# Expert down weights issued by ScalarE: a sparse-attention and mixture-of-experts step on one Trainium2 core

## What is computed

```python
def swiglu(x, w13, w2):
    a, b = jnp.split(x @ w13, 2, axis=-1)
    return (jax.nn.silu(a) * b) @ w2

    ...
    y = swiglu(h, w_sh13, w_sh2)
    for e in range(N_EXPERTS):          # 64
        y = y + combine[:, e:e + 1] * swiglu(h, w_exp13[e], w_exp2[e])
```

## Time and profile before

| | us |
|---|---|
| three runs | 1360.8, 1352.27, 1358.23 |
| median | 1358.23 |
| the profiled execution | 1353.77 |
| its span, first to last instruction | 1352.1 |

### The profile page before, as it was taken

One profiled execution on the slowest core, in us unless ns is written; L12 is line 12 of the kernel. 1 busy time (PEld: TensorE's weight loads), 2 busy tenths in 40 slices (PEclk: granted clock), 3 DMA queues, 4 the chain that ended last, 5 costly groups with the idle time before them and its releaser, 6 DMA issues. The chain is left out here.

```text
span 1352.1 us, 20742 instructions
## 1 busy us (share of the span) xinstructions
PE 1232.7 (91%) x7495; PEld 517.5 (38%) x7495; DVE 636.8 (47%) x1114; ACT 230.0 (17%) x496; POOL 453.8 (34%) x574
## 2 busy tenths in 40 slices
PE   5999889999999798999899998989989899988997
PEld 3545443444555544554232222222222222222343
DVE  1336579969971533674332222223323332221775
ACT  1024331021233310011011110111101101101211
POOL 5444416312244000154444343443434344431010
PEclk9999988999999898999999998999989999989899
DMA  8233220122111266024689999999999999997971
GB/s 281 60 112 106 65 82 9 63 74 86 24 25 24 83 234 261 35 70 167 244 333 415 402 415 411 399 412 395 415 388 412 398 405 399 413 408 270 400 176 54
DMA packets 98107, 318.65 MB, mean 236 GB/s; under 512 B 51642, under 2 KB 53438, under 8 KB 80025
## 3 DMA queue, kind: packets, MB, share of 16 engines
q1 hardware_dynamic: 74960, 269.94, 51.7%
q0 software_dynamic: 22960, 47.45, 10.1%
q10 hardware_dynamic: 96, 0.02, 0.0%
HBM read 298.70 MB, written 31.33 MB: 244 GB/s over the span
## 5 line engine op out<-in xcount | busy, mean ns | idle before, releaser
L1675 PE MATMUL ps<-arena 128*32 128x512 f32 x3072 | 355.4, 616 | 45.0 <-DMA arena<-in_w_exp 41.5
L2160 DVE STREAM_TRANSPOSE arena<-arena 128x1024 f32<-128x1024 f32 x48 | 100.0, 2083 | 253.9 <-DMA arena<-h_rows,arena 252.8
L997 POOL DMA_INDIRECT arena<-h_rows,arena x192 | 193.0, 1005 | 73.0 <-issue 72.1
L1675 PEld LDWEIGHTS ps<-arena 128*32 128x32 f32 x3072 | 97.6, 113 | 266.7 <-issue 214.3
L1688 PE MATMUL ps<-arena 128*32 128x512 f32 x1536 | 173.5, 592 | 0.8 <-DVE arena L2194 0.8
L1334 PE MATMUL ps<-arena 128*128 128x512 f32 (+1 forms) x384 | 166.5, 591 | 4.9 <-DMA arena<-in_w_in 4.8
L1056 ACT ACTIVATE arena<-ps 128x512 f32<-128x512 f32 (+5 forms) x226 | 102.5, 485 | 364.4 <-PE ps L1310 202.1
L1004 POOL DMA_INDIRECT y_rows<-arena x48 | 48.7, 1015 | 303.9 <-DVE arena L2194 289.1
L1334 PEld LDWEIGHTS ps<-arena 128*128 128x128 f32 x384 | 72.5, 192 | 91.4 <-issue 90.7
L1688 PEld LDWEIGHTS ps<-arena 128*32 128x32 f32 x1536 | 49.5, 110 | 115.5 <-issue 115.5
L1265 ACT ACTIVATE arena<-ps 128x256 f32<-128x256 f32 x48 | 18.4, 384 | 390.3 <-PE ps L1675 390.3
(11 more groups left out here) (237 smaller groups left out, 1294.3 us busy)
## 6 DMA issues: line engine op xcount, KB each, us to landing
arena<-in_w_exp SPq DMA_DIRECT2D x64, 2048.0 KB, 21.2
arena<-in_w_exp SPq DMA_DIRECT2D x64, 1024.0 KB, 15.8
arena<-in_w_in SPq DMA_DIRECT2D x6, 2048.0 KB, 8.0
arena<-y_rows SPq DMA_DIRECT2D x5, 2048.0 KB, 12.1
arena<-y_rows SPq DMA_DIRECT2D x5, 1024.0 KB, 7.9
arena<-in_x_prompt SPq DMA_DIRECT2D x8, 512.0 KB, 9.0
arena<-in_cache_v SPq DMA_DIRECT2D x128, 32.0 KB, 1.8
arena<-in_w_out SPq DMA_DIRECT2D x2, 2048.0 KB, 11.9
```

Source lines behind the costliest of these rows:

```text
L997: pool.indirect_dma_start(out=xg[s][:, 256 * g:256 * g + 256], out_offset=None, in_=h_quarters, in_offset=bass.IndirectOffsetOnAxis(ap=fro ...
L1675: ins = mm(ps[e % 3][q, :], xgT[e % 2][:, kk, q], w13[slots[g]][:, kk, :], start=(kk == 0), stop=(kk == KT - 1))
L2160: v.transpose(xgT[e % 2].rearrange("p c (g i) -> p g c i", g=4), xg[e % 3].rearrange("p (g j c) -> p g c j", g=4, c=KT)).then_inc(turned, 1)
```

## The change

`up_weights` and `down_weights` move up in the file so that two engines can use them. On SyncE, `load_expert` becomes `load_up`, which issues only the up weights; the first three main experts' down weights and the first kept one's are still issued there (those of the second kept expert too, by a line that did not change). On ScalarE, after its half of the y eviction of pass e, come the down weights of main expert e + 3, and in every third pass those of the next kept expert too. The slot is free then, because that eviction has waited for the down product of pass e. Instructions that compute are the same ones.

```diff
-            def load_expert(e, s, passes):
+            def load_up(e, s, passes):
                 if passes:
                     sp.wait_ge(up, passes)
                 sp.dma_start(*up_weights(e, s)).then_inc(w13_in[s], 16)
-                if passes:
-                    sp.wait_ge(down, passes)
-                sp.dma_start(*down_weights(e, s)).then_inc(w2_in[s], 16)
 
             def load_main(n):
-                load_expert(4 * (n // 3) + n % 3, main_slot(n)[0], n - 2 if n >= 3 else 0)
+                load_up(4 * (n // 3) + n % 3, main_slot(n)[0], n - 2 if n >= 3 else 0)
+                if n < 3:
+                    sp.dma_start(*down_weights(n, main_slot(n)[0])).then_inc(w2_in[main_slot(n)[0]], 16)
 
             def load_kept(q):
-                load_expert(4 * q + 3, kept_slot(q)[0], 3 * q - 3 if q >= 2 else 0)
+                load_up(4 * q + 3, kept_slot(q)[0], 3 * q - 3 if q >= 2 else 0)
+                if q < 1:
+                    sp.dma_start(*down_weights(3, kept_slot(q)[0])).then_inc(w2_in[kept_slot(q)[0]], 16)
...
                 copy(ye[e % 2][:, 0:512], ps[3 + 2 * (e % 2)][:, :], scale=gate[:, list_row(e):list_row(e) + 1]).then_inc(ya, 1)
+                if e + 3 < PASSES:
+                    slot = main_slot(e + 3)[0]
+                    act.dma_start(*down_weights(4 * ((e + 3) // 3) + e % 3, slot)).then_inc(w2_in[slot], 16)
+                if e % 3 == 2 and (e + 4) // 3 < PASSES // 3:
+                    q = (e + 4) // 3
+                    slot = kept_slot(q)[0]
+                    act.dma_start(*down_weights(4 * q + 3, slot)).then_inc(w2_in[slot], 16)
```

More of the change, by code:

```diff
@@ L713, in load_values, with up_weights, down_weights @@
             load_pages(eng, b, (("cache_v", lambda g: values[b // 4][:, bass.ds(b % 4 * NPG + g, 1), :][:, 0, :]),), v_in[b // 4])
+        def up_weights(e, s):
+            return w13[s], a["w_exp13"][0][e:e + 1].rearrange("a (p k) n -> p (a k) n", p=P)
+        def down_weights(e, s):
+            return w2[s], a["w_exp2"][0][e:e + 1].rearrange("a (p k) n -> p (a k) n", p=P)
         block = ctx.enter_context(nc.Block())
```

## The result

The changed kernel takes 1390.3 us (median), the kernel before 1355.72 us in the runs beside it: a ratio of 1.0261, 95% interval 1.0207 to 1.0315. The change makes the kernel 2.6% slower, outside the range of the prediction and on the side of its second rival. The profiled execution took 1388.8 us, 35.0 more than that of before.

The account below looks back on a forecast made before the run. DMA engines were taken to bound the passes, 11.95 us at best against 12.32. Passes at 12.14 give 7.6 us off; issue cost and starting lead count zero, so -8 us from 1358.23 gives 1350 us, range 1336 to 1378.

Parts of the forecast that it names:

- second rival: In the passes, gathers become the limit (d over 3.1): 1358 to 1435 us, mostly under 1378; chance 0.26.
- Issue cost: 59 down loads issued on ScalarE behind its y half fit under an up product of 6.89 us: zero.
- The price of a turn: At the DMA queues, a POOL packet beside both loaded weight queues takes 0.93 us a turn.
- The prediction's own sign of being wrong: In the passes, if gathers land past 15 us, the pass grows beyond 12.6 us.
- TensorE then waits about 1.3 us in every pass: TensorE waits this for VectorE, instead of 5 us in every third pass for weights.
- that goes: On TensorE, the slow up product after long weight waits, 8.73 us against 7.07, disappears, inside the same sum.
- 12.14: Forecast us a pass, taken as the middle between 12.33 and the floor of 11.95; 7.6 us off in 42 passes.
- d of 3.1: Gathers later by d us make a pass at least 11.3 + d/3; 3.1, the worst of three batches, gives 12.33.
- The loop of 33.9 us: Gather loop from scatter issue through transpose, turn, up, down and y half: 33.9 us for three passes, 11.3 a pass.
- hand layout: Queue loads laid out by hand for three passes at 12.4 us: d 3.1 for the worst batch, 0.9 for the mean.
- The whole bound of 8.8: Gathers 8.8 us later if both weight queues are always loaded: 14.2 us a pass, over 1435 us.
- The rule: Issuing DMAs from several engines saves issue time only: sum 0, time 1358 us; as the rival "nothing changes", chance 0.10.

Follow-up runs that it names:

- e1: The changed kernel with down loads given back to SyncE's queue, requests at the same moments: 1346.97 us, 0.992 of the kernel before; run again, 1346.59 us, 0.9938.
- filler: The changed kernel with 20 more transposes of a constant on TensorE ahead of the turn in every third pass: 1365.57 us, 1.0044 of the kernel before.
- e7: The one-queue kernel of e1 with weight loads in pieces of 4 KB a partition: 1364.44 us, 1.006 of the kernel before.

## Why the prediction was wrong

**Right.** The bound before was right: DMA engines with a floor of 11.95 us a pass and dips behind waits; e1 takes the dips and runs at 12.11. Issue cost nothing: ScalarE's copies lost 3.8 us to the issues in front of them, in 14 cases, and no engine waited for that. The waits on weights went altogether. The price of a turn held to 0.01 us, and gathers landed 4.5 us later. The prediction's own sign of being wrong came, gathers past 15 us (15.3) and a pass beyond 12.6 (13.05). The second rival named the mechanism, the place and the side.

**Wrong, the decisive step: "TensorE then waits about 1.3 us in every pass".** It waits 3.5 to 6.9 us in every third, and "that goes", said of the slow up product, did not come true: the slow up products moved from behind the weight waits to behind the late turns, and there are more of them. Behind the 14 late turns the up product takes 8.65 us on the mean to the next row (9.13 in the cycle above), against 6.89, and most of these turns take 0.19 more. 13 of them lie in the 42 passes: 25 us, and no term of the sum held it. The kernel before has 14 us of the same there, behind 8 weight waits, so of the 30.7 us that the change costs in these passes the clock has 11; against a forecast that put it at nothing it is all 25. The filler, which takes most of this away and leaves the late gathers, gives 1.0261 - 1.0044 of 1356 us back, 29 us, and 20.4 in the traces' 42 passes. I had the slow up products of the kernel before in the rows, and took it for granted that waits would spread.

**Wrong, the choice of 12.14.** It was the middle between the worst of three batches (d of 3.1, 12.33 a pass) and their mean (0.9). A batch's loop closes three passes later, on the batch of the same place in the cycle of kept loads. So the worst batch meets itself and sets the pace; the mean of the three has no part in it. The worst place, the first of the three above, has 22.3 us from scatter issue to transpose on the mean, for 18.5: d of 3.8. The loop of 33.9 us, this 3.8 and 1.9 for the slow up product and its turn make 39.6 for three passes, and from turn 7 to turn 43 three passes take 39.56 (754.21 to 1228.92). The three places' mean of 18.7 would have left d near nothing. The hand layout's worst case was nearly right, and the choice beside it was not: 12.33 for 12.14 is 8 us of the miss. With the clock's 25 that is 33 of the 38 us between 12.14 and 13.05 in 42 passes. The other 5 are what is left: d of 3.8 for 3.1, less the last passes, in which turn no longer waits.

**The rival's price.** For d of 4.4 it gave 1377. The measured d was smaller and the time 13 us longer, again for want of the clock's term. The whole bound of 8.8 was not reached; the rival's own reason, that a waiting TensorE asks for no weights, fits this, but no run shows it alone.

**The rule.** The Trainium skill ("DMA: Bandwidth & Descriptors", section "Issuing engines are not separate DMA queues") says that issuing from several engines saves issue time alone. The runs agree that it brings nothing else: e1 has the whole gain on one queue. But "nothing" would have been 1356 us, and it is 1390. The Trainium skill (the same page, section "Queues, rings and completion order") states that each DMA engine goes round the queues packet by packet; the 335, 362 and 390 packets agree, as far as counts can show it, and that sentence, not the first, carries the price of a third queue.

## What to carry to other kernels

Before a second engine issues transfers, ask who else stands at the DMA engines with small packets: here the third loaded queue added one of its packets to every turn, and reordering the issues on one queue brought the gain without that. Where a loop closes after as many passes as the cycle of loads has, the time is set by the worst place in the cycle, since it meets itself again, and not by the mean. A wait that moves to TensorE has to be priced with the work behind it, at the clock that the wait leaves.

## What was new about the hardware

Pieces of 4 KB a partition moved 395 GB/s with the DMA engines at 1.02, pieces of 8 and 16 KB 411 at 1.01 (e7, e1). Three loaded queues were served equally in packets, so the down queue with 2.70 MB and POOL's with 0.87 MB had as many turns in 20 us as the up queue with 4.70. And 20 transposes that compute nothing, 2.40 us in every third pass, made a kernel 2.2% faster: the mean granted clock from 700 to 1200 us was 0.98 with them and 0.93 without.
